# Nine row buffers, moved sums and states, and an early, partly split modulation product in a hybrid retention, Fourier and PEER layer

## The reference, cut to what matters

```python
mod_x = silu(c) @ w_ada + b_ada            # 6*1024 wide; the same with c_ctx
sh1, sc1, g1, sh2, sc2, g2 = split(mod_x, 6)
hc = rms(ctx)*(1 + csc1) + csh1            # context: keys and values only
hx = rms(x)*(1 + sc1) + sh1
q, k, v, gate, f = split(hx @ w_in)        # 8 heads of 64; rotary on q and k
# forward and backward retention in chunks of 128, first states from the context:
#   scores = q k' * decay_mask;  out = scores v + (q * q_decay) state
#   state  = state * chunk_decay + (k * k_decay)' v
# f: real part of a 2-D DFT over positions and channels
x = x + g1 * rms(concat(ret, four) @ w_out)
h2 = rms(x)*(1 + sc2) + sh2
# PEER: top 16 of 128 keys in each half for 8 heads, top 16 of 256 candidates,
# softmax weights w; act = h2 . u[ids];  out = sum w*gelu(act) * v[ids]
x = x + g2 * rms(peer(h2))
```

## Time and profile before

| | us |
|---|---|
| median of 3 runs | 1613.38 (1610.68 to 1614.76) |
| profiled execution | 1609.51 |
| its span | 1607.7 |
| PE busy | 1523.0 (95%) |
| DVE busy | 1229.9 (77%) |
| ACT busy | 578.0 (36%) |
| POOL busy | 412.6 (26%) |

### The profile page before, as it was taken

How to read it: one execution, slowest core, us unless ns; L and a number is a source line. 1 busy time by engine, 2 the same in 40 slices (tenths; PEclk the granted TensorE clock), 3 DMA queues, 4 the chain that set the end, 5 groups by cost and what they waited for, 6 DMA issues and landing times.

```text
span 1607.7 us, 21696 instructions
## 1 busy us (share of the span) xinstructions
PE 1523.0 (95%) x8105; PEld 1331.6 (83%) x8105; DVE 1229.9 (77%) x2337; ACT 578.0 (36%) x843; POOL 412.6 (26%) x336
## 2 busy tenths in 40 slices
PE   6899987979999999959999999999999999999997
PEld 1588867658899999959999999988888888888886
DVE  1776356775689978769999995567988888888885
ACT  3323150342223333324444444333433333333333
POOL 0000000000036787843222221121222222222211
PEclk9899998979999999979999999999999999999999
DMA  8388110312424788867999999999999999999971
GB/s 359 99 311 283 40 53 1 101 43 62 155 93 164 254 266 279 291 221 276 360 368 371 370 362 337 344 366 415 377 386 372 382 355 380 385 370 376 362 307 66
DMA packets 148005, 432.61 MB, mean 269 GB/s; under 512 B 13280, under 2 KB 46432, under 8 KB 144864
## 3 DMA queue, kind: packets, MB, share of 16 engines
q1 hardware_dynamic: 76896, 221.28, 37.8%
q0 software_dynamic: 36864, 134.23, 23.0%
q10 hardware_dynamic: 34176, 76.29, 12.5%
HBM read 377.22 MB, written 54.53 MB: 269 GB/s over the span
## 4 chain that ended last, share of the span: by engine, by line
PE 67%; DMA 5%; DVE 3%; POOL 2%; ACT 1%; issue 0%; ACTq 0%; DVEq 0%
PE ps L1561 21%; PE ps L1562 21%; PE ps L1563 21%; PE ps L1904 3%; DMA grp_w<-w_dram 2%; DMA rows<-u_nat,ids 1%; POOL ws_lo L557 1%; DMA blk_raw<-v_nat 1%; PE ps L1856 1%; DMA g_dram<-g_buf 1%; DVE rows L1367 0%; POOL rows L565 0%; ACT ws_hi L820 0%; DVE ps L1403 0%; DVE ps L1399 0%
## 5 line engine op out<-in xcount | busy, mean ns | idle before, releaser
L1561 PE MATMUL ps<-hT_hi,ws_hi 128*128 128x384 f32 (+1 forms) x1184 | 413.9, 350 | 7.9 <-POOL ws_lo L557 6.4
L1562 PE MATMUL ps<-hT_lo,ws_hi 128*128 128x384 f32 (+1 forms) x1184 | 407.0, 344 | 0.0
L1563 PE MATMUL ps<-hT_hi,ws_lo 128*128 128x384 f32 (+1 forms) x1184 | 406.9, 344 | 0.0
L1561 PE MATMUL ps<-vs_hi,coef_hi 128*128 128x512 f32 x768 | 299.0, 389 | 3.8 <-DVE coef_lo L1529 3.8
L1562 PE MATMUL ps<-vs_lo,coef_hi 128*128 128x512 f32 x768 | 298.8, 389 | 0.0
L1563 PE MATMUL ps<-vs_hi,coef_lo 128*128 128x512 f32 x768 | 298.8, 389 | 0.0
L820 ACT ACTIVATE ws_hi<-blk_raw 128x1024 fp32r<-128x1024 f32 x128 | 135.7, 1060 | 337.6 <-PE ps L1563 337.1
L1561 PEld LDWEIGHTS ps<-hT_hi,ws_hi 128*128 128x128 f32 x1184 | 224.3, 189 | 16.9 <-POOL ws_lo L557 5.1
L874 ACT ACTIVATE vs_hi<-blk_raw 128x1024 fp32r<-128x1024 f32 x128 | 135.6, 1060 | 276.8 <-PE ps L1563 263.2
L1563 PEld LDWEIGHTS ps<-hT_hi,ws_lo 128*128 128x128 f32 x1184 | 224.0, 189 | 6.5
L1562 PEld LDWEIGHTS ps<-hT_lo,ws_hi 128*128 128x128 f32 x1184 | 224.4, 190 | 5.8
(11 more groups left out here) (284 smaller groups left out, 1823.8 us busy)
## 6 DMA issues: line engine op xcount, KB each, us to landing
blk_raw<-u_t SPq DMA_DIRECT2D x128, 512.0 KB, 5.8
blk_raw<-v_nat SPq DMA_DIRECT2D x128, 512.0 KB, 7.3
g_dram<-g_buf ACTq DMA_DIRECT2D x128, 192.0 KB, 4.9
w_dram<-w_stage SPq DMA_DIRECT2D x48, 512.0 KB, 8.8
grp_g<-g_dram ACTq DMA_DIRECT2D x15, 1536.0 KB, 9.9
grp_w<-w_dram ACTq DMA_DIRECT2D x15, 1536.0 KB, 25.4
part_w<-w_ada SPq DMA_DIRECT2D x32, 512.0 KB, 6.3
raw<-w_in SPq DMA_DIRECT2D x20, 512.0 KB, 7.2
```

Source lines behind the costliest of these rows:

```text
L1561: pe.matmul(o, lh, rh, start=start, stop=False, skip_group_check=True)
L1562: pe.matmul(o, lh, rl, start=False, stop=False, skip_group_check=True)
L1563: return pe.matmul(o, ll, rh, start=False, stop=stop, skip_group_check=True)
```

## The change

1. **Start.** Two chunks of w_ada are loaded ahead of x. Chunks 4 to 7 are rounded by ACT and their rests taken by DVE, and PE multiplies them in split form: 12 single-pass matmuls for a chunk in place of 4 in f32. The rest of unit 0 is taken before the modulation is known; in piece 0 PE goes slice by slice over all six row blocks and waits for one slice at a time; DVE takes a slice's rest right behind its modulation. The decay tables and masks are made by DVE at the very start, their exponentials on ACT after piece 0. The first load of a `part_w` waits for the first product's end.
2. **Sums.** The 32 one-column products are spread between the row blocks of units 1 to 3 of piece 3.
3. **States.** Weighted keys are made after piece 3's units on DVE; `states(0)` and `states(1)` go ahead of units 1 and 2 of piece 4, the two scans behind the rests of units 18 and 19; units 16 to 19 use two slots. All key and query transposes come after piece 4. The DFT tables are rounded during piece 4. Scores 0 to 2 follow the Fourier groups at once, and outputs stand earlier among the scores.
4. **Rows.** Nine buffers for the first 36 rows, a new planner, the exponential one block later, and PE's wait for the weights before block 53 in place of after it; the wait for the converted picks stands behind the products of block 54.
5. **First group.** The three weight pieces are issued at blocks 119, 121 and 124.

```diff
-EXP_AT = PART_A - 4
+EXP_AT = PART_A - 3
+G_EARLY = 9
+FIRST_W_AT = (EB - 9, EB - 7, EB - 4)
+def row_slot(k):
+    return k % (G_EARLY if k < FIRST_ROWS else G_RING)
+def row_behind(k):
+    return max([i for i in range(k) if row_slot(i) == row_slot(k)], default=None)
 def gathers_at():
-    third = [21 + 5 * k // 4 for k in range(sum(SEARCH_ROWS[2]))]
-    used = third + [36 + k for k in range(sum(SEARCH_ROWS[3]))] + [PART_A - 1] * EARLY_ROWS
+    used = [19 + 5 * k // 4 for k in range(third)] + [34 + k for k in range(sum(SEARCH_ROWS[3]))]
+    used += [PART_A - 2] * EARLY_ROWS + [b for b in range(PART_A, EB + V_ACT) for _ in range(act_rows(b))]
...
+        due = max(14 + k, used[k] - 5)
+        behind = row_behind(k)
+        first.append(due if behind is None else max(due, used[behind] + 2))
...
+            def ada_split(kc):
+                pe.wait_ge(ada_l, kc - ADA_WHOLE + 1)
+                for n in range(4):
+                    last = split_mm(ps[0:2, n, :], csil_hi[:, kc, :], csil_lo[:, kc, :], ada_hi[kc % 4 % 3][:, col],
+                                    ada_lo[kc][:, col], False, kc == KC - 1)
...
-            for kc in range(4):
+            for kc in range(ADA_WHOLE):
                 ada_chunk(kc)
             pe.wait_ge(ident_ld, 16)
             pe.wait_ge(xn_done, 6)
             for kc in range(4):
                 transposed(kc)
-            ada_chunk(4)
-            ada_chunk(5)
+            pe.wait_ge(silu_done, 3)
+            ada_split(4)
+            ada_split(5)
...
+                    if p == 4 and j in (1, 2):
+                        states(j - 1)
...
+                        if p == 3 and j:
+                            i = TB * (j - 1) + tb
+                            sum_parts(i * parts // (3 * TB), (i + 1) * parts // (3 * TB))
...
             for h in range(3):
                 score(h)
+            outputs(0)
             score(3)
             score(4)
-            states(1)
+            outputs(1)
             score(5)
-            outputs(0)
             score(6)
+            pe.wait_ge(four_l, GROUPS)
+            sum_squares(0)
+            outputs(2)
             score(7)
...
-            with pe.Fori(1, PART_A // 2) as i:
+            with pe.Fori(1, PART_A // 2 - 1) as i:
                 for p in range(2):
                     products(2 * i + p, p, 2 * i + (p - 1))
+            products(PART_A - 2, 0, PART_A - 3)
             pe.wait_ge(soft_step, 3)
...
-            pe.wait_ge(ptr_taken, 3)
+            products(PART_A - 1, 1, PART_A - 2)
             def part(j, blk, q, free):
                 products(blk, j % 2, blk - 1)
+                if j == 0 and free is None:
+                    pe.wait_ge(ptr_taken, 3)
```

More of the change, by code:

```diff
@@ L53 @@
 SPLIT = 4
+ADA_WHOLE = 4
 PART_RING = 4
@@ L1036, in _, with rope @@
             rsteps = [0]
-            def rope_all(t, kind):
-                for tb in range(TB):
+            def rope(t, kind, tbs):
+                for tb in tbs:
                     s = tb % 2
@@ L1063, in _ @@
                 for j in range(4 if 0 < p < n_proj else 0):
+                    if p == 4 and j == 2:
+                        dve.wait_ge(proj_taken, 20)
+                        rope(q_sb, 0, range(2))
+                    if p == 4 and j == 3:
+                        scan(0)
                     rest_unit(4 * p + j)
                     add_parts(4 * p + j - 3)
+                    if p == 4 and j == 3:
+                        rope(q_sb, 0, range(2, TB))
+                        scan(1)
                     if p == 4 and j == 0:
@@ L1589, in _ @@
                 transposed(kc)
-            ada_chunk(4)
-            ada_chunk(5)
+            pe.wait_ge(silu_done, 3)
+            ada_split(4)
+            ada_split(5)
             for kc in range(4, KC):
                 transposed(kc)
-            ada_chunk(6)
-            pe.wait_ge(ada_in[KC - 1], 16)
-            for n in range(4):
-                last = pe.matmul(ps[0:2, n, :], csil[:, KC - 1, :], ada_w[KC - 1][:, n * 512:(n + 1) * 512],
-                                 start=False, stop=True)
-            last.then_inc(ada_done, 1)
+            ada_split(6)
+            ada_split(7)
             pe.wait_ge(rows_out, 2)
@@ L1666, in _ @@
                     last.then_inc(split_used, 1)
+            pe.wait_ge(rope_step, 5 * TB)
+            pe.wait_ge(st_taken, 4 * TB)
+            for m in range(4):
+                transpose_pair(m)
             pe.wait_ge(rope_step, 10 * TB)
@@ L1704, in _ @@
             dft2(3)
-            def states(d):
-                pe.wait_ge(ckw_done, 4)
-                pe.wait_ge(kw_done, (TB - 1) * (d + 1))
-                if d:
-                    pe.wait_ge(st_taken, 2 * TB)
-                for c2 in range(PAIRS):
-                    col = slice(c2 * P, (c2 + 1) * P)
-                    for jb in range(CB):
-                        pe.matmul(ps[:, 1, col], ck_w[:, d, jb, col], cv_sb[:, jb, col], start=jb == 0,
-                                  stop=jb == CB - 1)
-                for n in range(TB - 1):
-                    for c2 in range(PAIRS):
-                        col = slice(c2 * P, (c2 + 1) * P)
-                        last = pe.matmul(ps[:, 3 + 2 * n, col], k_w[:, d, n, col],
-                                         v_sb[:, n if d == 0 else TB - 1 - n, col], start=True, stop=True)
-                last.then_inc(st_done, 1)
             def score(h):
```

370 lines of the change are left out of this document (212 added, 158 removed).

## The result

| | before | after |
|---|---|---|
| median | 1612.03 us (1609.61 to 1614.76, 4 runs) | 1587.84 us (1586.89 to 1588.48, 4 runs) |
| profiled execution, its span | 1609.51, 1607.7 us | 1587.41, 1585.6 us |

The ratio is 0.9849 (95% interval 0.983 to 0.9868): faster, by 24 us by the medians. The profiled spans differ by 22.1 us. To see where they went I took one mark for each stage from PE's timeline in both traces; the columns are the time from one mark to the next.

The account below looks back on a forecast made before the run. PE was taken as the bound, busy 1523.0 of 1607.7 us, so only its idle or low-clock places could give time. 6.5 + 4.0 + 13.5 + 26.4 + 1.5 = 51.9; 1613.4 - 51.9 = 1561.5 us, range 1550 to 1578.

Parts of the forecast that it names:

- Term 1: Start to first projection matmul: two chunks ahead of x, split chunks and slice-wise projection gain 6.5 us, ends 3 and 9.
- my later case: Start: if the clock falls after PE idles for chunk 2, the product ends near 49.4 us, not 46.4.
- DVE's rests then pace chunks 4 to 7: Start: after the four transposes, DVE's rests pace chunks 4 to 7 at 2.7 us each in split form.
- waits for the parts: Projection: first part load goes out 2 to 4 us later; part sums must be complete 11 us earlier.
- 9 us are left: Piece 3: sums needed at 154.9 us before the shift, last part sum ended at 145.9, leaving 9 us.
- Term 2: One-column sums spread between row blocks in piece 3: 11.9 us in place of 15.9, gain 4.0, ends 2 and 5.
- Term 3: States, scores and outputs, from piece 4 to the output projection: gain 13.5 us, ends 9 and 17.
- Rival B: Front gains little: clock falls before chunk 2 and the output projection, start and states give 10, not 20; 1571 us, chance 0.2.
- Term 4: Rows, block 0 to the one-hots: earlier gathered rows stop DVE's and PE's waits, gain 26.4 us, ends 14 and 28.
- 54 blocks need 224.7 us: Rows stage: blocks pace at 4.16 us, so 54 need 224.7, where block 54 starts 251.5 after block 0.
- Rival A: Rows stay late: wait moves to the exponential or POOL's pace, half the rows' gain comes; 1575 us, chance 0.15.
- Term 5: First group, before the second product: weight pieces issued at other blocks shorten waits, gain 1.5 us, ends 0 and 3.5.

Follow-up runs that it names:

- The edit of the queue alone: Changed kernel with each w_in unit loaded ahead of the part_w pieces that stood before it on SP's queue: 1579.91 us, ratio 0.9784.

## Why the prediction was wrong

**Term 1, start: 3.7 for 6.5.** From the product's end to the first projection matmul I gave 5.2 and it took 5.4 (50.46 to 55.85). The product ended at 50.5, a microsecond past my later case. Chunk 2 came after 4.75 us of idle PE and not 3.4, and the clock fell behind it. What I did not see is a second stop of 2.81 us before chunk 4: DVE takes four context columns, the last at 32.17, before the chunk's rest:

```profile
32.17 0.42 DVE L1065 COPY cxT<-ps 128x256 f32<-128x256 f32 x1 [0.23 <-PE ps L1657]
32.52 6.68 DVE L1069 TENSOR_TENSOR ada_lo<-ada_w,ada_hi 128x2048 fp32r<-128x2048 f32 x3
```

"DVE's rests then pace chunks 4 to 7" was right in kind; that the first rest stands behind the last copy was left out. The clock fell behind this stop as well. The next projection matmuls recovered 1.5 us (6 slow ones in place of some 14), but that is lost again at once:

**The failed step of terms 1 and 2** is the sentence on "waits for the parts". It followed the part loads only to the sums ("9 us are left", and they were left: the last part sum ended at 149.2 and PE came at 158.1) and not to what stands behind the part loads in SP's queue: w_in's units. The later first load itself (50.6 in place of 44.8) was not what held them: SP then waited 23.2 us for DVE's first part sum, which came at 75.61 in place of 73.02, behind the last slice of the modulation. So unit 7's load went out at 89.92 in place of 88.0, while PE was 3.7 us earlier. Before, ACT's rounding of that unit waited for PE (until 95.34) and not for the load, so the late load was hidden, by little. Afterwards it stopped PE for 6.1 us and cost 2.2 at 1.2 GHz. The edit of the queue alone gave 7.9 us.

Term 2 itself, 4.0, gave 3.0 from piece 2 to piece 4 (50.95 us in place of 53.94). The mechanism was right and its size a little off: behind each group of one-column products the next six full matmuls took 1.45 to 1.49 us in place of 1.37, some 1.2 us over the 12 groups, which the term had only in its ends. Putting the block back cost 6.0, since the clock fell earlier in it.

**Term 3: 11.3 for 13.5.** The first output product came 67.5 us after piece 4's start; 66.3 was forecast. The inverse chain left 3.47 + 0.78 idle where I wrote 3.5. The clock behind it was named and priced at 3 "half the time". It came, and it cost 2.3 of the 3.3 us that the next stage lost. Here the mechanism was right and the size within its ends. Rival B, which priced terms 1 and 3 together at 10, came near: they gave 3.7 + 11.3 = 15.0, or 11.7 less the next stage's 3.3, and the clock did fall at both places that it names. The front's largest loss, in the queue, it did not have.

**Term 4: 16.9 for 26.4.** The step that failed is "54 blocks need 224.7 us", 4.16 each. ACT's gelus of blocks 2 and 42 in the changed kernel stand 169.7 us apart, and 40 blocks at 4.16 are 166.4:

```profile
468.56 0.47 ACT L884 ACTIVATE g_buf<-ps 128x384 f32<-128x384 f32 x1
...
638.24 0.47 ACT L884 ACTIVATE g_buf<-ps 128x384 f32<-128x384 f32 x1
```

In the kernel before it is the same (476.14 and 645.89), so those 3.3 us were never the rows' to give; I had read the pace from the quietest stretch. Three gathers in a block cost 3.7 us over three blocks where I counted 1. And the exponential's move a block later, which I costed inside the chain at nothing, is worth 2.6 us at the one-hot products and 4.2 in the whole. That is 3.3 + 2.7 + 2.6 = 8.6 of the 9.5 missing. Only the last of the three is shown by a run at that size: the first is read from the timelines of both kernels, and of the second's 2.7 the run with the gathers spread gave back 1.0 at the one-hot products. DVE ended its rows 222.0 us after block 0 (676.5), not the 216.4 of my count, but the exponential, at 681.5, was later still. The rest was right: rows' wait 12.3 for "some 10", weights' wait 1.6 for 0 to 3, POOL's rest at 2.47. Rival A (the wait moves to the exponential or to POOL's pace) is what happened, at three quarters of its price of 13, though the rows themselves were not late.

**Term 5: 2.9 for 1.5**, within its ends: PE waits 1.1 us for the first coefficients in place of 3.5.

**The end: 5.2 us that no term held.** That it comes with the ninth row buffer, and that it is POOL's last DRAIN outlasting the store, is shown; why the DRAIN takes 11.6 us is not.

**The range.** Seven of the eight stages fell short and one went over. The ends of the single terms were taken as independent; but, as I read it, each was the middle of a mechanism followed along one engine, and what was left out on the others could only cost.

## What to carry to other kernels

When work moves earlier, list what stands behind each moved or delayed load in its queue, and check the date of every one of them, not of the moved load's own user alone; a stream that was late but hidden is the first thing that a gain exposes. Read a pace over the whole stage and not over its best stretch. Where one engine's chain is shortened, look at once at the next in line, here an exponential a block too late, which cost 4 us and a one-character edit.

## What the hardware showed that I had not expected

- The end of the span: 5.2 us more with nine buffers for gathered rows than with six or eight, whatever the length of PE's program and the count of semaphores. It is POOL's DRAIN at the end of its program, 11.6 us with nine, 5.7 with six and 3.1 with eight, and it shows only where it outlasts the last store. Whether the buffers, their own semaphores or the gathers that use them make it was not tried.
- A small DVE instruction can last as long as the POOL instruction beside it. The copy of the last tokens' weights took 2.28 us next to a rest on POOL, and 0.23 in the kernel with six buffers, where no rest ran:

```profile
683.72 2.51 POOL L589 TENSOR_TENSOR ws_lo<-blk_raw,ws_hi 128x1024 fp32r<-128x1024 f32 x1 [0.67 <-ACT ws_hi L877]
684.03 2.28 DVE L1505 COPY sp_w<-picks 128x128 f32<-128x128 f32 x1
```

```profile
688.77 0.23 DVE L1505 COPY sp_w<-picks 128x128 f32<-128x128 f32 x1
```

  Both end within 0.1 us of each other (686.23 and 686.31). The Trainium skill (SBUF — State Buffer, "Who interferes with whom") speaks of a port pair that one of the two locks for a whole instruction; the rows agree, and here it was DVE that waited, in the very chain that sets the one-hots.
- A block of 64 one-column records keeps PE busy and still loses the clock, after about 2.5 us of them where the block was put back into the changed kernel, 5.5 in the kernel before and 3.8 in the kernel before with unused semaphores.
